# Which of a tile's 128 slots the tokens of an expert occupy: from the middle outwards in place of from the first slot up

## The reference, cut to what matters

```python
g_idx = jnp.argmax(g_logits, axis=-1)                    # one of 8 groups
top_p, top_i = lax.top_k(e_prob, TOP_K)                  # 2 of the 8 experts in it
expert_id = (g_idx[:, None] * EXPERTS_PER_GROUP + top_i).reshape(-1)
order = jnp.argsort(expert_id)
xs = ht[tok]                                             # tok = order // TOP_K
gate = lax.ragged_dot(xs, w_gate, group_sizes)           # 64 experts, 1024 x 256 each
up = lax.ragged_dot(xs, w_up, group_sizes)
y = lax.ragged_dot(silu(gate) * up, w_down, group_sizes) # 256 x 1024 each
out = jnp.zeros_like(ht).at[tok].add(y * weights)
```

## Time and profile before

| | us |
|---|---|
| median of 3 runs | 2124.54 (2122.97 to 2125.74) |
| profiled execution, first to last instruction | 2126.7 |
| TensorE busy with matmuls | 1956.5 (92%) |
| DVE busy | 808.6 (38%) |
| ACT busy | 615.9 (29%) |
| POOL busy | 606.6 (29%) |

### The profile page before, as it was taken

The page is one execution under the profiler, slowest core; times in us unless marked ns, Lnnn a source line. Parts: engine busy times, 40 slices in busy tenths (PEclk is TensorE's granted clock), DMA queues, the critical chain, the costliest instruction groups (busy, mean ns, idle before and its releaser), DMA issues. The chain is left out here.

```text
span 2126.7 us, 31150 instructions
## 1 busy us (share of the span) xinstructions
PE 1956.5 (92%) x12049; PEld 1379.7 (65%) x12049; DVE 808.6 (38%) x1461; ACT 615.9 (29%) x1324; POOL 606.6 (29%) x619
## 2 busy tenths in 40 slices
PE   8999999999999989999999899999979888888885
PEld 7998887787787767878887666666563222322222
DVE  5223256666453443440112456676531211111114
ACT  5333145555323432331112432232212111111111
POOL 1226387332211110010114676665211111111102
PEclk9999999999999999999999999999989989999998
DMA  5103461211420253622332422211659999999996
GB/s 208 52 31 140 147 200 26 51 26 46 150 83 28 45 122 67 83 60 94 94 119 86 161 83 95 81 56 55 260 224 417 425 424 425 423 422 420 418 383 263
DMA packets 101730, 371.80 MB, mean 175 GB/s; under 512 B 17429, under 2 KB 40154, under 8 KB 74714
## 3 DMA queue, kind: packets, MB, share of 16 engines
q1 hardware_dynamic: 82592, 323.55, 42.6%
q0 software_dynamic: 16704, 42.10, 5.1%
q10 hardware_dynamic: 2298, 4.23, 0.5%
HBM read 321.47 MB, written 65.14 MB: 182 GB/s over the span
## 5 line engine op out<-in xcount | busy, mean ns | idle before, releaser
L2907 PE MATMUL ps<-w_gu,rows_t 128*64 128x512 f32 x1024 | 260.4, 667 | 58.1 <-DMA w_gu<-w_up 56.5
L2907 PEld LDWEIGHTS ps<-w_gu,rows_t 128*64 128x64 f32 x1024 | 79.2, 152 | 216.1 <-issue 155.8
L3165 POOL DMA_INDIRECT y_d<-y_out,asg_i x32 | 32.2, 1006 | 429.9 <-DVE y_out L2991 414.7
L2982 DVE TENSOR_TENSOR act_s<-act_g,ps 128x256 f32<-128x256 f32 x32 | 13.5, 421 | 326.1 <-ACT act_g L2973 326.1
L2334 PE MATMUL ps<-w_o,mix_t 128*128 128x512 f32 x256 | 124.3, 616 | 0.0
L2925 PE MATMUL ps<-w_d,act_tt 128*64 128x512 f32 x512 | 116.9, 598 | 0.5 <-issue 0.5
L1120 ACT ACTIVATE prob<-ps,stats 128x1024 f32<-128x1024 f32 (+7 forms) x128 | 94.5, 738 | 62.1 <-DVE stats L1083 61.7
L2973 ACT ACTIVATE act_g<-ps 128x256 f32<-128x256 f32 x32 | 12.3, 384 | 323.7 <-PE ps L2907 323.7
L310 PE MATMUL ps<-tk_lo,h_hi 128*128 128x512 f32 x256 | 100.4, 392 | 3.0 <-DVE tk_lo L302 3.0
L310 PE MATMUL ps<-tk_hi,h_lo 128*128 128x512 f32 x256 | 100.3, 392 | 0.0
L310 PE MATMUL ps<-tk_hi,h_hi 128*128 128x512 f32 x256 | 100.2, 392 | 0.0
(11 more groups left out here) (477 smaller groups left out, 4389.6 us busy)
## 6 DMA issues: line engine op xcount, KB each, us to landing
w_gu<-w_gate SPq DMA_DIRECT2D x64, 1024.0 KB, 20.0
w_gu<-w_up SPq DMA_DIRECT2D x64, 1024.0 KB, 23.5
w_d<-w_down SPq DMA_DIRECT2D x64, 1024.0 KB, 23.6
w_tk<-w_in SPq DMA_DIRECT2D x5, 2048.0 KB, 13.6
proj_d<-tok_o POOLq DMA_DIRECT2D x40, 256.0 KB, 2.3
tk_in<-proj_d SPq DMA_DIRECT2D x8, 1280.0 KB, 5.9
w_ch<-w_in SPq DMA_DIRECT2D x12, 512.0 KB, 10.2
proj_d<-conv_o POOLq DMA_DIRECT2D x12, 512.0 KB, 3.9
```

The lines of the kernel that those rows point to most:

```text
L2907: mm = pe.matmul(ps[half, 2, :].rearrange("p (g n) -> p g n", g=2), rows_t[:, k, half], w_gu[q][:, h, :, k, :], start=(k == 0), stop=(k == ...
L2982: v.tensor_tensor(act_s[:, :].rearrange("q (k p) -> q k p", k=2), by_k(act_g[:, :]), by_k(ps[:, 2, DE:]), ALU.mult).then_inc(s_acts, 1)
L3165: pool.indirect_dma_start(out=y_d, out_offset=bass.IndirectOffsetOnAxis(ap=idx, axis=0), in_=y_out[q][:, :], in_offset=None, bounds_check= ...
```

## The change

The slots are filled from the middle of the tile outwards: an even expert's assignments take slots 63, 62, 61 and so on, an odd expert's 64, 65, 66. Ranks of even experts are made negative (`r_side` is -1 for even experts and +1 for odd ones), and the row they are compared with is no longer `iota` but `r_slot`, which is slot - 63 for slots 0 to 63 and the slot's own number above. The two rows are made once, at the beginning of the delta net stage. In the tables for further pairs the absolute value of `r_sel` is taken first. `eb_row` moves to a region of memory that is free in the experts' stage, to make room.

```diff
-        eb_row = take("eb_row", [1, P], dt=I32)
+        r_side, r_slot = take("r_side", [P, EXPERTS]), take("r_slot", [P, P])
...
                 link(v.scalar_tensor_tensor(rank, flat4(r_over[:, :, :]), NOWHERE, b, ALU.mult, ALU.add), "rank", t)
                 v.sem_inc(bank_free[place["RK", t][0]], 1)
+                link(v.tensor_tensor(rank, rank, r_side[:, :], ALU.mult), "side", t)
...
-                    link(v.tensor_scalar(ohs[k][:, :], const("iota"), r_sel[:, a:a + 1], const("asg")[:, a:a + 1], ALU.is_equal, ALU.mult), f"h{k}", t)
+                    link(v.tensor_scalar(ohs[k][:, :], r_slot[:, :], r_sel[:, a:a + 1], const("asg")[:, a:a + 1], ALU.is_equal, ALU.mult), f"h{k}", t)
...
                 v.tensor_scalar(flat4(r_sum[:, :, :]), const("limit"), 1.0 / P, -0.5, ALU.mult, ALU.add).then_inc(s_sum0, 1)
-                v.wait_ge(s_sum0, 1)
+                v.tensor_scalar(r_side[:, :], const("limit"), 2.0 / HB, -3.0, ALU.mult, ALU.add).then_inc(s_sum0, 1)
+                v.tensor_scalar(r_slot[:, :], const("iota"), float(HB), 1.0 - HB, ALU.is_lt, ALU.mult).then_inc(s_sum0, 1)
+                v.wait_ge(s_sum0, 3)
+                v.tensor_tensor(r_slot[:, :], r_slot[:, :], const("iota"), ALU.add).then_inc(s_sum0, 1)
+                v.wait_ge(s_sum0, 4)
...
-        for _name, _count in (("n", 4), ("nt", 1), ("end", 4), ("eb", 5), ("at", 10)):
+        for _name, _count in (("n", 4), ("nt", 1), ("end", 4), ("eb", 5), ("at", 11)):
...
-                link(stt(x_pos[:, :], x_pos[:, :], EXPERTS * HB - NOWHERE, r_sel[:, :], ALU.add, ALU.add))
+                link(stt(x_at[:, :], r_sel[:, :], -1.0, r_sel[:, :], ALU.mult, ALU.max))
+                link(stt(x_pos[:, :], x_pos[:, :], EXPERTS * HB - NOWHERE, x_at[:, :], ALU.add, ALU.add))
```

More of the change, by code:

```diff
@@ L2060, in build @@
         pool_l = Count("l_pool", "ms rs"); act_l = Count("l_act", "sq"); dve_l = Count("l_dve", "hn")
-        dve_r = Count("r_dve", "log gmax gd val mx oh prod es m1 v1 x1 o1 e2 m2 v2 x2 o2 a0 a1 m over rank s0 s1 h0 b0 h1 b1 sum")
+        dve_r = Count("r_dve", "log gmax gd val mx oh prod es m1 v1 x1 o1 e2 m2 v2 x2 o2 a0 a1 m over rank side s0 s1 h0 b0 h1 b1 sum")
         act_r = Count("r_act", "exp")
@@ L2822, in build @@
         x_col = take("x_col", [P, N_MORE], 2)
+        eb_row = take("eb_row", [1, P], dt=I32)
         y_d = dram("y_d", (2 * S, D))
```

## The result

| | us |
|---|---|
| before, median of 6 runs | 2124.56 (2121.40 to 2125.74) |
| with the change, median of 6 runs | 2131.07 (2128.70 to 2133.68) |
| ratio | 1.0032, 95% interval 1.0022 to 1.0042 |
| profiled execution of the change, its span | 2132.81, 2131.1 |

The change makes the kernel slower by 0.32%, some 6.5 us, where +2.1 was forecast. The time is inside the range, but by the prediction's own bound of 0.2% it is "slower", to which it gave 0.16, and not "the same".

The account below looks back on a forecast made before the run. DMA engines were taken to bound the experts' stage, with DVE's stream getting a new instruction in the delta net loop. 0 + 0.8 + 1.3 = +2.1 us on 2124.5 gave 2126.6 us; own range 2123.5 to 2129, stated range 2122.5 to 2131.5.

Parts of the forecast that it names:

- Term 1: Experts' stage: the new slots leave the heaviest DMA engine its 186 rows, so 0; bounds -7.1 and 0 us.
- assignment (b): Gathers and scatters: slots in groups of four, 32 apart on one engine, lower and upper 64 on eight engines each.
- Rival A: Experts' stage: slots 16 apart share an engine, so the change is faster, -5.0 us in all, 2119.5 us; chance 0.06.
- rival D: Experts' stage: slots don't decide the engine at all, term 0 as forecast; chance inside the forecast's 0.81.
- Term 2: Delta net loop and last tiles: one more DVE product per tile lengthens TensorE's waits, 0.8 + 1.3 us.
- above, 5 x 0.44 = 2.2 us: Upper bound on the loop's five waits for u_fin, with the 0.18 us behind r_rank paid a second time.
- rival B: Delta net loop: r_sum, moved later, is shut out by POOL's L2772; +4.5 us on the sum, 2131.1 us; chance 0.10.
- Terms 3 and 4: Three instructions at the beginning, hidden by DVE's wait for ACT, and the tables for further pairs: 0 each.
- Rival C: Experts' stage: the engine that becomes heavy is slow; at 2% slower +5.7 us, 2132 us with other terms; chance 0.03.

Follow-up runs that it names:

- the slots alone: The change's slots without its product in the loop, the sign put in the row that ranks are compared with: 2125.18 us, ratio 1.0002 to before.
- balanced slots: Kernel before, no product, with each expert's ranks dealt out over the eight groups of four slots of its half: 2115.69 us, ratio 0.9956.
- the product alone: Kernel before plus one product per tile of r_rank with a row of ones, slots and tables unchanged: 2129.11 us, ratio 1.0022.
- before with the same idle turns: Kernel before with extra TensorE transposes filling its waits in four loop steps and the last tiles: 2123.36 us, ratio 0.9988.
- two products: The change with a second product per tile, with ones, behind the first: 2137.42 us, ratio 1.0062 to before.

## Why the prediction was right or wrong

*Term 1, the slots: right.* 0 was forecast; the pairs are 395.4 apart in place of 395.9, and the slots alone have a ratio of 1.0002. The reason is shown too: assignment (b) gave the sign and, within 0.9 us, the size for balanced slots. The Trainium skill, "DMA: Bandwidth & Descriptors", "The descriptor swizzle", states this assignment; the runs bear it out for gathers and scatters with one index per partition (-7.9 and +21.0 us where it wants -8.8 and +16.3). Rival A (slots 16 apart) and rival D (slots decide nothing) are refuted by the same two kernels: A wants +5.0 in the distance for both, D wants 0.

*Term 2, the product: this is the step that failed, by its size.* It was put at 3 x 0.26 + 5 x 0.26 = 2.1 us; by the medians the change cost 6.5 us, and the product alone 4.7. Each piece came as forecast: L2263 waits 6.3 us in five, for `r_sum` TensorE waits 2.11, 3.02 and 1.92 (forecast 2.15, 3.07, 1.97), each full-clock step grew by 0.25. By the net column, against before with the same idle turns, one product costs 1.1, 2.4, 1.7 and 1.5 us, and two cost 3.0 and 2.8. What the sum left out is a second price of the same wait. The prediction took a longer idle time of TensorE as costing its own length. It costs the granted clock as well: 3.2 us for each long stretch at 1.2 GHz that it brings into the loop, in some steps and not in others. In the profile of the change "low" is up by 5.2 us, 3.4 in the loop and 1.8 in the last tiles, where the measured stretch is 6.2 us longer. The 3.4 are on the path, as the starts of L2263 show; how much of the 1.8 is, no run shows. Over all runs it is 6.0 us of "low". The bound "above, 5 x 0.44 = 2.2 us" was a bound on instructions only.

That the time lies in the stated range is luck. Its upper end of 2131.5 us was set by the price of rival B, which did not happen; the forecast's own range ended at 2129.

The profile of before held the warning. Its clock is 0.91 from 1,500 to 1,600 us (the row above), where TensorE waits 1.71 to 2.81 us for `r_sum`; in the loop, where it waits 1.23 us, the clock is full. Whether a wait that grows from the one towards the other could cost clock was never asked.

*Terms 3 and 4: right.* The three instructions stand ahead of a wait for ACT that is now 3.85 us in place of 4.42, and the slots alone, which have four of them, have a ratio of 1.0002.

*Rival B: its price, 2131.1 us, is the time measured, and its mechanism did not happen.* `r_sum` takes 0.22 to 0.23 us in all eight tiles, where B wanted over 1. In three of the steps it starts 0.12 to 0.13 us behind POOL's L2777, as B had it (1448.44 behind 1448.31 in the step shown). POOL's power instruction does not shut DVE out. The rule of the Trainium skill, "SBUF — State Buffer", "SBUF: two separate sides", holds here beside POOL's large product (2.13 us for L2646 in place of 0.23) and not beside the power instruction. A time that agrees shows nothing on the mechanism; the row does.

*Rival C:* under (b) the last of the lower engines now has 174 rows, and the distance did not grow. It had 3.7 us in hand, so a slowness below 0.8% stays possible; the 2% of the rival's price would have shown.

"If the stage before the experts is later by more than 4 us, the reasoning is wrong" was the right alarm: it was 7.5 us later, 6.2 of it behind the first long wait for `u_fin`.

## What to carry to other kernels

Cost an instruction on a waiting path twice: by its length, and by what it does to TensorE's idle time, if waits a little longer are followed by half clock elsewhere in the same profile. A cheap test is to fill that wait with idle turns and leave all else alone; if the time and the granted clock come back together, it was the clock. And where a transfer leaves rows out, look which engine the full rows lie on: dealing them out was worth 9.5 us here and moved no byte, while mirroring one half was worth nothing, because the heaviest engine kept its rows.

## What the hardware showed that I had not expected

- One instruction of 0.25 us per tile, eight in all, costs 4.7 us (ratio 1.0022); the change with a second one is 13.0 us above before.
- An idle time of 1.2 us in the loop is followed by full clock throughout in two of the four profiles that have it, and by one short half-clock stretch in each of the other two. Idle times of 1.3 to 1.7 us are followed by a stretch of nearly 7 us in three of eleven steps and by none in the other eight (the change, the product alone, two products). What decides was not found.
- Half clock in the last tiles is mostly off the path: 6.8 us less of it shortened the stretch by 2.2 us, because DVE's `hn` came no earlier.
